# Tokens gathered for two experts at once, in 256 columns, between the down products of the expert before

## The chip, the cores and the metric

The kernel runs on one core of a Trainium2 chip. The metric is device time in microseconds (us), the median of a few executions. Everything is float32 at the interface.

## What is computed

Four transformer layers over 256 tokens of 1024 values. Only the last layer's feed-forward part is touched by the change: a mixture of eight experts, of which each token takes two.

```python
def swiglu(x, w13, w2):
    a, g = jnp.split(x @ w13, 2, axis=-1)
    return (jax.nn.silu(a) * g) @ w2

def moe_ffn(x, router_w, router_b, w13, w2):
    logits = (x @ router_w).astype(jnp.float32) + router_b.astype(jnp.float32)
    top_v, top_i = lax.top_k(logits, TOP_K)
    wts = jax.nn.softmax(top_v, axis=-1)
    gate = jnp.einsum('bsk,bske->bse', wts, jax.nn.one_hot(top_i, N_EXPERTS, dtype=jnp.float32)).astype(x.dtype)
    y = jnp.zeros_like(x)
    for e in range(N_EXPERTS):
        y = y + gate[..., e:e + 1] * swiglu(x, w13[e], w2[e])
    return y
```

An expert's weights are 1024 x 7168 and 3584 x 1024.

## The kernel before

**Precision.** Every operand of a product is split into a high part and a rest, both fp32r. ScalarE writes the high part (`wh`, L1042), VectorE subtracts it from the raw weights (`wl`, L1427), and `t_mm3` (L443 to L445) multiplies high by high, high by rest and rest by high. SyncE loads the weights in slots of 1024 KB (L2239) into a ring of five buffers; three sets of `wh`/`wl` follow one another. Each set is written when the products of the slot three places earlier are done.

**An expert.** The router finds which tokens go to which expert, and each token's place among that expert's at most 128. The kernel gathers the tokens of an expert with a 0/1 matrix: `X` (256 tokens, split into XH and XL, stationary) times `SELR` (128 columns, one for each place, moving) gives the tokens' transpose in PSUM, and ScalarE copies it to `GH` and `GL`. So for each expert TensorE does 8 groups of 128 features x 2 halves of the tokens x 2 parts = 32 matmuls of 128 columns. Then:

- the hidden products, 7 chunks of 512 columns with 4 slots each (12 matmuls of 512 columns in a slot). After a chunk, `turn` transposes the chunk before (4 transposes, L629), and one entry of the list `between` runs;
- the down products, 14 slots, accumulated in two PSUM banks that are held all that time;
- the scatter of the result back to the tokens (`t_scatter`, 2 x 4 matmuls of 512 columns with `SELT`, the transpose of `SEL`), in the first two chunks of the next expert.

**The order** is written out by hand for each engine. `t_experts` (L996) fills `between` for expert e with the scatter of e-1 (chunks 0 and 1), an empty entry, and four pieces of the gather for e+1: 8 matmuls each, after chunks 3 to 6 (1 to 4 in expert 0). The last one also transposes `SEL` (L982, 2 transposes). ScalarE (`a_gather`, L1366) and VectorE (`v_gather`, L2072; both 0/1 matrices of an expert are written in one chunk by `v_choose`, L2065) have lists of the same length. The gather for expert 0 stands alone between the router and the first product, followed by `t_most`, 4 small matmuls. `GH`, `GL`, `SEL`, `SELR` and `SELT` are doubled, by e modulo 2.

**The banks.** `Groups.take` (L164) hands out the eight PSUM banks in turn and makes TensorE wait until the bank's last contents were read:

```python
g = self.n
self.n += 1
self.number[key] = g
if g >= 8:
    engine.wait_ge(self.out_sem[g % 8], g // 8)
return self.banks[g % 8]
```

A second page of experts (for more than 128 tokens at one expert) stands behind a branch that these inputs don't take.

## Time and profile before

| | |
|---|---|
| median of 3 runs | 2379.91 us (2378.08 to 2380.12) |
| the profiled execution's own time | 2378.64 us |
| its span | 2377.2 us |
| TensorE busy | 2330.3 us (98%), weight loads 2002.4 us |
| VectorE busy | 1743.6 us (73%) |
| ScalarE busy | 1375.3 us (58%) |
| read from memory | 577.42 MB |
| chain that ended last | PE 88%, DVE 7%, all others 1% or less |

The own time of the profiled execution is 1.4 us above its span and 1.3 us below the median. Busy shares are means over stages: the eight experts take from 1376 to 2360 us of the span. PE is TensorE, PEld its weight loads, DVE VectorE, ACT ScalarE, SP SyncE.

### The profile page before, as it was taken

To read this page: it belongs to the slowest core of one execution; us is meant where nothing else is said; L and a number is where in the kernel's file an instruction comes from. 1 tells how busy PE (TensorE), PEld (TensorE's weight loads), DVE (VectorE), ACT (ScalarE), POOL (GpSimd) and SP (SyncE) were. 2 spreads that over 40 slices of the span, in tenths; PEclk is the share of its full clock that TensorE was granted. 3 is DMA by queue.
4 is the path that set the end of the run, shared out by engine and by line. 5 is a ranking of instruction groups with operands and counts; after the bars stand their busy time and mean duration, and the time that the engine had idled before them with its cause. 6 is when DMAs were issued, how large, how long until landed. Compare 5 with 4: busy or idle time off the path is not lost.

```text
span 2377.2 us, 31162 instructions
## 1 busy us (share of the span) xinstructions
PE 2330.3 (98%) x12658; PEld 2002.4 (84%) x12658; DVE 1743.6 (73%) x2248; ACT 1375.3 (58%) x1797; POOL 75.8 (3%) x91
## 2 busy tenths in 40 slices
PE   8999999999999999999999899999999999999997
PEld 6898888898888999788899888888888888888885
DVE  6757555857555458655655888989898989899997
ACT  5455444554443444444344367777777777777774
POOL 3100001300000000000000000000000000000000
PEclk9999999999999999999999989999999999999999
DMA  7335554426554534555333489999899989898995
GB/s 249 142 142 202 181 194 142 176 72 239 195 181 152 182 120 178 190 182 200 133 124 109 175 332 359 361 353 364 349 368 347 368 347 377 350 370 345 367 363 187
DMA packets 94167, 580.59 MB, mean 244 GB/s; under 512 B 21776, under 2 KB 23104, under 8 KB 24768
## 3 DMA queue, kind: packets, MB, share of 16 engines
q1 hardware_dynamic: 92704, 572.15, 64.1%
q10 hardware_dynamic: 1312, 6.37, 0.7%
q8 instruction: 102, 1.67, 0.3%
q14 instruction: 49, 0.40, 0.0%
HBM read 577.42 MB, written 1.06 MB: 243 GB/s over the span
## 4 chain that ended last, share of the span: by engine, by line
PE 88%; DVE 7%; DMA 1%; ACT 1%; POOL 1%; issue 1%; SPq 0%; DVEq 0%; POOLq 0%
PE bank L443 26%; PE bank L445 26%; PE bank L444 26%; PE bank L440 7%; DVE wl L1427 3%; PE bank L629 2%; DMA raw<-in_ws 1%; PE bank L675 1%; POOL SM L2143 1%; DVE L L1679 1%; ACT wh L1042 1%; DVE X L1526 0%; DVE GT L1741 0%; DVE SM L1459 0%; DVE X L1471 0%
## 5 line engine op out<-in xcount | busy, mean ns | idle before, releaser
L1427 DVE TENSOR_TENSOR wl<-raw,wh 128x1024 fp32r<-128x1024 f32 x706 | 830.8, 1225 | 233.8 <-ACT wh L1042 232.1
L1042 ACT ACTIVATE wh<-raw 128x1024 fp32r<-128x1024 f32 x706 | 706.4, 1054 | 341.0 <-PE bank L445 299.2
L443 PE MATMUL bank<-wh,GH 128*128 128x512 f32 x896 | 352.1, 393 | 0.0
L445 PE MATMUL bank<-wh,GL 128*128 128x512 f32 x896 | 349.5, 390 | 0.0
L444 PE MATMUL bank<-wl,GH 128*128 128x512 f32 x896 | 349.5, 390 | 0.0
L1427 DVE TENSOR_TENSOR wl<-spare,wh 128x1024 fp32r<-128x1024 f32 x264 | 309.9, 1221 | 22.4 <-ACT wh L1042 21.9
L1042 ACT ACTIVATE wh<-spare 128x1024 fp32r<-128x1024 f32 x264 | 264.5, 1054 | 65.0 <-PE bank L445 65.0
L443 PE MATMUL bank<-wh,HH 128*128 128x512 f32 (+1 forms) x768 | 290.8, 379 | 11.3 <-DVE HL L1442 5.7
L444 PE MATMUL bank<-wl,HH 128*128 128x512 f32 (+1 forms) x768 | 288.3, 375 | 0.0
L445 PE MATMUL bank<-wh,HL 128*128 128x512 f32 (+1 forms) x768 | 287.8, 375 | 0.0
L443 PE MATMUL bank<-HH,wh 128*128 128x256 f32 x896 | 257.4, 287 | 1.7 <-DVE HL L1983 1.7
L445 PE MATMUL bank<-HH,wl 128*128 128x256 f32 x896 | 253.5, 283 | 0.0
L444 PE MATMUL bank<-HL,wh 128*128 128x256 f32 x896 | 253.4, 283 | 0.0
L445 PEld LDWEIGHTS bank<-wh,GL 128*128 128x128 f32 x896 | 168.6, 188 | 35.7
L443 PEld LDWEIGHTS bank<-wh,GH 128*128 128x128 f32 x896 | 168.7, 188 | 34.2
L444 PEld LDWEIGHTS bank<-wl,GH 128*128 128x128 f32 x896 | 168.8, 188 | 34.0
L443 PEld LDWEIGHTS bank<-wh,HH 128*128 128x128 f32 x768 | 146.4, 191 | 40.3 <-issue 8.7
L443 PEld LDWEIGHTS bank<-HH,wh 128*128 128x128 f32 x896 | 171.7, 192 | 5.7 <-issue 2.9
L443 PE MATMUL bank<-wh,EH 128*128 128x512 f32 x448 | 175.8, 392 | 0.0
L445 PE MATMUL bank<-wh,EL 128*128 128x512 f32 x448 | 174.5, 389 | 0.0
L444 PE MATMUL bank<-wl,EH 128*128 128x512 f32 x448 | 174.3, 389 | 0.0
L444 PEld LDWEIGHTS bank<-HL,wh 128*128 128x128 f32 x896 | 171.8, 192 | 0.1
(241 smaller groups left out, 3343.4 us busy)
## 6 DMA issues: line engine op xcount, KB each, us to landing
raw<-in_ws SPq DMA_DIRECT2D x353, 1024.0 KB, 5.1
spare<-in_ws SPq DMA_DIRECT2D x132, 1024.0 KB, 5.9
more<-in_ws SPq DMA_DIRECT2D x48, 1024.0 KB, 4.8
once<-in_ws SPq DMA_DIRECT2D x4, 1024.0 KB, 11.3
QT<-in_relb SPq DMA_DIRECT2D x4, 768.0 KB, 12.5
LNB<-in_ln ACTq DMA_DIRECT2D x3, 1024.0 KB, 4.6
LNB<-in_ln ACTq DMA_DIRECT2D x4, 512.0 KB, 3.5
raw<-in_ws SPq DMA_DIRECT2D x2, 816.0 KB, 4.6
```

What stands on the lines that cost most here:

```text
L440: return T.q.matmul(o, l, r, start=start, stop=stop)
L443: T.q.matmul(o, l[0], r[0], start=start, stop=False)
L444: T.q.matmul(o, l[0], r[1], start=False, stop=False)
L445: return T.q.matmul(o, l[1], r[0], start=False, stop=stop)
L629: ins = T.q.transpose(room[:, 128 * k:128 * k + 128], TU[t][:, 128 * k:128 * k + 128], ident)
L675: ins = T.q.transpose(room[:, 128 * n:128 * n + 128], LB[t][:, 256 * h + 128 * i:256 * h + 128 * i + 128], ident)
L1042: A.q.activation(sets[c % NSET][0][:, half * i:half * i + half], raws[stream.place[n]][:, half * i:half * i + half], ACT.Copy).then_inc(*h ...
L1427: V.q.tensor_tensor(wl[:, half * i:half * i + half], raw[:, half * i:half * i + half], wh[:, half * i:half * i + half].bitcast(f32), ALU.s ...
L1679: ins = V.q.tensor_tensor_reduce(L[:, 256 * h:256 * h + n], room[:, 256 * i:256 * i + n], bias(h), 1.0, NEG if sinks is None else sinks[:, ...
L2143: return G.q.tensor_tensor(o, x, PW[:, 0:x.shape[1]], ALU.pow)
```

## The change

- `t_gather(p)` gathers for the pair of experts 2p and 2p+1 side by side. The moving operand is 256 columns of `SELR`, both experts' matrices next to one another: 32 matmuls of 256 columns for a pair, in eight pieces of 4, each filling one bank.
- For pairs 1 to 3 the pieces stand in the down products of the odd expert ahead of them, one after each of the slots 2 to 9 (`between` of `t_down`). ScalarE copies a piece (128x2x2x128 now) after it has split the slot behind. The hidden products carry no gather.
- `SEL` is transposed for two experts at once (`t_turn_sel`, 4 transposes), in a chunk of the even expert.
- VectorE writes the four 0/1 matrices of a pair one per chunk, in chunks 2 to 5 of the odd expert before. For pair 0 all four are written ahead of expert 0.
- `GH`, `GL`, `SEL`, `SELR`, `SELT` are single arrays that hold a pair, of the same size in all.
- `Groups` counts the uses of each bank, and `skip(2)` lets the ring step over the two banks held by the down products before the sixth piece.

```diff
@@ class Groups
-        self.number, self.n, self.emptied = {}, 0, []
+        self.number, self.at, self.uses, self.emptied = {}, 0, [0] * 8, []
+    def again(self):
+        self.at, self.uses = 0, [0] * 8
+    def skip(self, n):
+        self.at += n
     def take(self, engine, *key):
-        g = self.n
-        self.n += 1
-        self.number[key] = g
-        if g >= 8:
-            engine.wait_ge(self.out_sem[g % 8], g // 8)
-        return self.banks[g % 8]
+        b = self.at % 8
+        self.at += 1
+        self.number[key] = b, self.uses[b]
+        if self.uses[b]:
+            engine.wait_ge(self.out_sem[b], self.uses[b])
+        self.uses[b] += 1
+        return self.banks[b]
     def bank(self, *key):
-        return self.banks[self.number[key] % 8]
+        return self.banks[self.number[key][0]]
...
@@ t_down
                     t_free(s_, full(name, i, tiles - 1, 1))
                 if k0 == 0 and after_first:
                     after_first()
+                if 2 <= k0 // 2 < 2 + len(between):
+                    between[k0 // 2 - 2]()
...
@@ t_gather, t_turn_sel, t_experts
-        def t_gather(e):
-            i = e % 2
-            def move(v, src, c4):
-                room = groups.take(T, "ga", e, v, c4)
+        def t_gather(p):
+            def move(c2, v):
+                room = groups.take(T, "ga", p, v, c2)
                 for t in range(2):
-                    T.wait_ge(*(tokens_in.at(t) if v else part.at("xs", t)))
-                    T.wait_ge(*selr.at(e, t))
-                for c in range(4 * c4, 4 * c4 + 4):
+                    T.wait_ge(*((tokens_in if v else part).at(*([t] if v else ["xs", t]))))
+                    for i in range(2):
+                        T.wait_ge(*selr.at(2 * p + i, t))
+                for j in range(2):
                     for t in range(2):
-                        a = 1024 * t + 128 * c
-                        ins = t_mm(room[:, 128 * (c % 4):128 * (c % 4) + 128], src[:, a:a + 128],
-                                   SELR[i][:, 128 * t:128 * t + 128], t == 0, t == 1)
-                ins.then_inc(*groups.fill("ga", e, v, c4))
-            def last():
-                move(1, XL, 1)
-                room = groups.take(T, "sel", e)
+                        a = 1024 * t + 256 * c2 + 128 * j
+                        ins = t_mm(room[:, 256 * j:256 * j + 256], (XL if v else XH)[:, a:a + 128],
+                                   SELR[:, 256 * t:256 * t + 256], t == 0, t == 1)
+                ins.then_inc(*groups.fill("ga", p, v, c2))
+            return [lambda c2=c2, v=v: move(c2, v) for c2 in range(4) for v in range(2)]
+        def t_turn_sel(p):
+            room = groups.take(T, "sel", p)
+            for i in range(2):
                 for t in range(2):
-                    T.wait_ge(*select.at(e, t))
-                    ins = T.q.transpose(room[:, 128 * t:128 * t + 128], SEL[i][:, 128 * t:128 * t + 128], ident)
-                ins.then_inc(*groups.fill("sel", e))
-            return [lambda: None, lambda: move(0, XH, 0), lambda: move(0, XH, 1), lambda: move(1, XL, 0), last]
+                    T.wait_ge(*select.at(2 * p + i, t))
+                    a = 256 * i + 128 * t
+                    ins = T.q.transpose(room[:, a:a + 128], SEL[:, a:a + 128], ident)
+            ins.then_inc(*groups.fill("sel", p))
         def t_scatter(e, t):
-            i = e % 2
-            w = SELT[i][:, 128 * t:128 * t + 128]
-            T.wait_ge(*out("sel", e))
+            a = 256 * (e % 2) + 128 * t
+            w = SELT[:, a:a + 128]
+            T.wait_ge(*out("sel", e // 2))
             for h in range(2):
                 room = groups.take(T, "sca", e, t, h)
                 T.wait_ge(*out("dn", ("e", e), 0, h))
...
                 t_mm(room[:, :], w, YL[:, 512 * h:512 * h + 512], False, True).then_inc(*groups.fill("sca", e, t, h))
         def t_experts(page):
-            for go in t_gather(8 * page):
+            for go in t_gather(4 * page):
                 go()
             if page == 0:
                 t_most()
             for e in range(8 * page, 8 * page + 8):
-                between = []
+                between, later = [], []
                 if e % 8:
                     between += [lambda t=t: t_scatter(e - 1, t) for t in range(2)]
-                if e % 8 < 7:
-                    between += t_gather(e + 1)
-                turn = t_swiglu(expert_slot(e), GV[e % 2], lambda k, t: out("ga", e, 1, k // 4),
+                if e % 2 == 0:
+                    between += [lambda: t_turn_sel(e // 2)]
+                elif e % 8 < 7:
+                    later = t_gather(e // 2 + 1)
+                    sixth = later[5]
+                    def past():
+                        groups.skip(2)
+                        sixth()
+                    later[5] = past
+                turn = t_swiglu(expert_slot(e), GV[e % 2], lambda k, t: out("ga", e // 2, 1, k // 2),
                                 E_CHUNKS, 1, ("e", e), between)
-                t_down(expert_slot(e) + 28, EV, lambda k, t: out("tu", ("e", e), k // 4, 0), 28, "dn", ("e", e), 1, turn)
+                t_down(expert_slot(e) + 28, EV, lambda k, t: out("tu", ("e", e), k // 4, 0), 28, "dn", ("e", e), 1, turn,
+                       between=later)
...
@@ a_gather, a_experts
-        def a_gather(e):
-            i = e % 2
-            def move(v, dst, c4):
-                a_copy(dst[i][:, 512 * c4:512 * c4 + 512], ("ga", e, v, c4), 512)
-            def last():
-                move(1, GL, 1)
-                a_copy(SELT[i][:, :], ("sel", e), 256)
-            return [lambda: None, lambda: move(0, GH, 0), lambda: move(0, GH, 1), lambda: move(1, GL, 0), last]
+        def a_gather(p):
+            def move(c2, v):
+                A.wait_ge(*full("ga", p, v, c2))
+                A.q.activation((GL if v else GH)[:, :].rearrange("p (i c n) -> p c i n", i=2, c=8)[:, 2 * c2:2 * c2 + 2],
+                               groups.bank("ga", p, v, c2)[:, :].rearrange("p (c i n) -> p c i n", c=2, i=2), ACT.Copy,
+                               scale=1.0).then_inc(*groups.empty("ga", p, v, c2))
+            return [lambda c2=c2, v=v: move(c2, v) for c2 in range(4) for v in range(2)]
...
                 for j in range(14):
                     a_hi(expert_slot(e) + 28 + j + 2)
                     if j == 0:
                         turn()
+                    if 3 <= j < 3 + len(later):
+                        later[j - 3]()
...
@@ v_choose, v_gather
-        def v_choose(e, dst, mark):
+        def v_choose(e, mark):
+            p = e // 2
             V.wait_ge(*out("pos"))
-            for t in range(2):
-                V.q.tensor_scalar(dst[:, 128 * t:128 * t + 128], CST[:, C_ROW:C_ROW + 128], 128.0 * (e // 8) + 1.0,
+            if p:
+                V.wait_ge(*(out("ga", p - 1, 1, 3) if mark is selr else out("sel", p - 1)))
+            for t in range(2):
+                if mark is selr:
+                    dst = SELR[:, 256 * t + 128 * (e % 2):256 * t + 128 * (e % 2) + 128]
+                else:
+                    dst = SEL[:, 256 * (e % 2) + 128 * t:256 * (e % 2) + 128 * t + 128]
+                V.q.tensor_scalar(dst, CST[:, C_ROW:C_ROW + 128], 128.0 * (e // 8) + 1.0,
                                   POS[:, 8 * t + e % 8:8 * t + e % 8 + 1], ALU.add, ALU.is_equal).then_inc(*mark.mark(e, t))
-        def v_gather(e):
-            i = e % 2
-            def choose():
-                v_choose(e, SELR[i], selr)
-                v_choose(e, SEL[i], select)
-            return [choose] + [lambda: None] * 4
...
@@ v_experts
-                if e % 8 < 7:
-                    between += v_gather(e + 1)
                 if e == 0:
-                    between[1] = v_gates_end
+                    between += [lambda: None, v_gates_end]
+                if e % 2 and e % 8 < 7:
+                    between += [lambda x=x, m=m: v_choose(x, m) for m in (selr, select) for x in (e + 1, e + 2)]
```

In the hunks the functions of the same name stand in the order of the file; blank lines are left out.

**Where the instructions now stand.** First TensorE between the router and expert 0. Before:

```order
L440 MATMUL bank<-SM,CST 128x8 x3
L440 MATMUL bank<-SELR_82,XH 128x128 x16
L440 MATMUL bank<-SELR_82,XL 128x128 x16
L982 MATMUL bank<-CST,SEL_80 128x128 x2
L440 MATMUL bank<-SM,CST 128x8 x2
L443 MATMUL bank<-wh,GH_76 128x512
```

Now:

```order
L446 MATMUL bank<-SM,CST 128x8 x3
L446 MATMUL bank<-SELR,XH 128x256 x4
L446 MATMUL bank<-SELR,XL 128x256 x4
...
L446 MATMUL bank<-SM,CST 128x8 x2
L449 MATMUL bank<-wh,GH 128x512
L450 MATMUL bank<-wl,GH 128x512
```

Of the second and third row there are four each, in turns. The gather still has 32 matmuls, of twice the columns, and the transposes of `SEL` are no longer ahead of the first product.

Second, TensorE in the hidden products of expert 1, where a chunk ends. Before:

```order
L443 MATMUL bank<-wh,GH_77 128x512
L444 MATMUL bank<-wl,GH_77 128x512
L445 MATMUL bank<-wh,GL_79 128x512
L629 MATMUL bank<-CST,TU_63 128x128 x4
L440 MATMUL bank<-SELR_82,XH 128x128 x8
L443 MATMUL bank<-wh,GH_77 128x512
```

Now, at the end of such a chunk:

```order
L449 MATMUL bank<-wh,GH 128x512
L450 MATMUL bank<-wl,GH 128x512
L451 MATMUL bank<-wh,GL 128x512
L637 MATMUL bank<-CST,TU_63 128x128 x4
L449 MATMUL bank<-wh,GH 128x512
```

and in its down products, at the end of slot 2:

```order
L451 MATMUL bank<-wh,EL 128x512
L446 MATMUL bank<-SELR,XH 128x256 x4
L449 MATMUL bank<-wh,EH 128x512
L450 MATMUL bank<-wl,EH 128x512
L451 MATMUL bank<-wh,EL 128x512
```

The block of 8 has left the chunk; a block of 4 stands directly between products of 512 columns.

Third, VectorE in expert 1, chunks 2 and 3. Before:

```order
L1442 TENSOR_TENSOR EL<-bank,EH 128x512
L2069 TENSOR_SCALAR SELR_82<-CST,SM 128x128 x2
L2069 TENSOR_SCALAR SEL_80<-CST,SM 128x128 x2
L1576 TENSOR_TENSOR TU_63<-TT_60,bank 128x512
L1427 TENSOR_TENSOR wl<-raw,wh 128x1024 x6
```

Now:

```order
L1461 TENSOR_TENSOR EL<-bank,EH 128x512
L2097 TENSOR_SCALAR SELR<-CST,SM 128x128 x2
L1595 TENSOR_TENSOR TU_63<-TT_60,bank 128x512
L1446 TENSOR_TENSOR wl<-raw,wh 128x1024 x6
L1446 TENSOR_TENSOR wl<-spare_82,wh 128x1024 x2
```

Four writes in one chunk became two in each of four chunks.

## Rows read from the trace of the kernel before

**Rows 1.** Waits, 1380 to 2370 us: engine line <- releaser: total us, times, longest

```profile
ACT wh L1042 <- PE bank L445: 165.4, 235, 2.6
...
SPq L2239 <- DVE wl L1427: 852.5, 325, 18.2
```

**Rows 2.** Busy time by stretch: us, PE, PEld, DVE, ACT, POOL (instructions); clock; DMA share; GB/s

```profile
1510.44:1633.59 123.15, 123.15 (x575) 102.60 (x575) 111.57 (x109) 94.36 (x105) 0.00 (x0) 1.00 0.95 360
...
2249.19:2357.50 108.31, 108.31 (x492) 89.64 (x491) 96.60 (x92) 78.79 (x87) 0.00 (x0) 1.00 0.84 321
...
1364.00:1380.00 16.00, 14.40 (x60) 13.52 (x60) 12.27 (x27) 4.74 (x9) 0.00 (x0) 0.51 1.01 424
```

**Rows 3.** Timeline of TensorE, experts 6 and 7: start us, us, engine, line, operation

```profile
2126.04 0.39 PE L440 MATMUL bank<-YH,SELT 128*128 128x512 f32 x1
...
2238.09 0.39 PE L445 MATMUL bank<-wh,EL 128*128 128x512 f32 x1
...
2249.19 0.39 PE L440 MATMUL bank<-YH,SELT 128*128 128x512 f32 x1
...
2357.51 0.39 PE L445 MATMUL bank<-wh,EL 128*128 128x512 f32 x1
```

**Rows 4.** Timeline of TensorE where products of 256 and 512 columns meet

```profile
1174.75 0.39 PE L445 MATMUL bank<-wh,HL 128*128 128x512 f32 x1
1174.97 0.28 PE L443 MATMUL bank<-HH,wh 128*128 128x256 f32 x1
1175.09 0.28 PE L444 MATMUL bank<-HL,wh 128*128 128x256 f32 x1
...
183.60 0.40 PE L443 MATMUL bank<-wh,MH 128*128 128x512 f32 x1
...
184.99 0.39 PE L443 MATMUL bank<-wh,MH 128*128 128x512 f32 x1
```

**Rows 5.** Timeline of TensorE: small matmuls in a row at the full clock

```profile
1545.70 0.60 PE L629 MATMUL bank<-CST,TU 128*128 128x128 f32 x4
1546.05 1.09 PE L440 MATMUL bank<-SELR,XH 128*128 128x128 f32 x8
...
862.63 3.62 PE L440 MATMUL bank<-U,raw 128*128 128x256 f32 x16
```

**Rows 6.** Timeline, router to expert 0

```profile
1367.72 0.48 DVE L2069 TENSOR_SCALAR SELR<-CST,SM 128x128 fp32r<-128x128 f32 x2
1368.12 1.22 DVE L2017 TENSOR_TENSOR XL<-X,XH 128x1024 fp32r<-128x1024 f32 x1
...
1368.35 3.65 PE L440 MATMUL bank<-SELR,XH 128*128 128x128 f32 x16 [0.95 <-DVE SELR L2069]
...
1369.64 4.63 DVE L1427 TENSOR_TENSOR wl<-raw,wh 128x1024 fp32r<-128x1024 f32 x4
...
1375.21 0.65 PE L982 MATMUL bank<-CST,SEL 128*128 128x128 f32 x2
1375.65 0.86 PE L440 MATMUL bank<-SM,CST 128*128 128x8 f32 x4
1376.36 0.77 PE L443 MATMUL bank<-wh,GH 128*128 128x512 f32 x1
...
1380.08 0.40 PE L443 MATMUL bank<-wh,GH 128*128 128x512 f32 x1
```

**Rows 7.** Busy time by stretch of 1 us: where the clock rises

```profile
1171.00:1172.00 1.00, 1.00 (x4) 0.79 (x4) 0.00 (x0) 0.00 (x0) 0.00 (x0) 0.74 0.12 41
...
1374.00:1375.00 1.00, 1.00 (x7) 1.00 (x6) 0.87 (x5) 0.34 (x1) 0.00 (x0) 0.50 1.03 434
...
1379.00:1380.00 1.00, 1.00 (x4) 0.79 (x3) 1.00 (x2) 0.00 (x0) 0.00 (x0) 0.64 1.02 426
```

**Rows 8.** Timeline before that rise, and VectorE in chunk 2 of expert 1

```profile
1167.63 0.77 PE L443 MATMUL bank<-wh,HH 128*128 128x512 f32 x1 [1.85 <-DVE HL L1442]
...
1536.20 0.47 DVE L2069 TENSOR_SCALAR SELR<-CST,SM 128x128 fp32r<-128x128 f32 x2
```

More of the change, by code:

```diff
@@ L2031, in v_router @@
             V.q.tensor_tensor(POS, groups.bank("pos")[:, 0:16], sm["se"], ALU.mult).then_inc(*groups.empty("pos"))
-            v_choose(0, SELR[0], selr)
+            for e in range(2):
+                v_choose(e, selr)
             v_tokens(1)
-            v_choose(0, SEL[0], select)
+            for e in range(2):
+                v_choose(e, select)
             v_lo(expert_slot(0) + 1)
@@ L2090, in v_experts @@
             if page:
-                for go in v_gather(8 * page):
-                    go()
+                for e in (8, 9):
+                    v_choose(e, selr)
+                for e in (8, 9):
+                    v_choose(e, select)
             for e in range(8 * page, 8 * page + 8):
```

36 lines of the change are left out of this document (19 added, 17 removed).

## The prediction

> **What bounds the kernel now.** The page says that TensorE is busy 98% of the span and has 88% of the chain that ended last, but that is a mean over stages, so I read the experts by themselves. First the waits of that stage [rows 1]. ScalarE waits 165.4 us in 235 waits for a product to free a weight set, the longest 2.6 us; SyncE waits 852.5 us for VectorE to free a buffer. Both run ahead of TensorE. No wait of TensorE is of any size. Then the stretches [rows 2]: from one scatter to the next, 123.15 us, TensorE is busy for all of it at the full clock, VectorE 111.57 us, the DMA engines 95%. So in the experts whatever TensorE no longer issues comes off the time, as long as VectorE, ScalarE and the DMAs keep up. Expert 7 is the test of that, since it has nothing to gather: TensorE is busy without a gap there too. Last I read how tightly small matmuls follow one another [rows 3 to 5], and the start of expert 0 [rows 6, 7], which runs at half the clock.
>
> **Part 1, gather and transposes leave seven experts.** From the first scatter to the last down product, expert 6 takes 2238.09 - 2126.04 = 112.05 us and expert 7 takes 2357.51 - 2249.19 = 108.32 us [rows 3]. They differ by four gather blocks and the two transposes of `SEL`: 3.73 us. Experts 0 to 6 each have them: 7 x 3.73 = **26.1 us removed**. One block takes nearly 0.9 us, as its 8 matmuls follow at (1.09 - 0.28) / 7 = 0.116 us [rows 5].
>
> **Part 2, pieces in the down products.** A piece is 4 matmuls of 256 columns between products of 512. The rows show all three steps [rows 4]: the first 256-column matmul starts 0.22 us after a 512-column one, as another 512 would; 256-column ones follow each other at 0.12 us; and six intervals of 512 after such a stretch take 184.99 - 183.60 = 1.39 us, 0.03 above six times 0.227. So twice the columns cost hardly more than 0.116, and a piece adds 4 x 0.12 + 0.03 = 0.51 us; I take 0.52. The bounds: 4 x 0.116 = 0.46 below; above, 0.60, if a piece leaves the product behind it late by 0.1. With 3 pairs x 8 pieces: 24 x 0.52 = **12.5 us added** (11.1 to 14.4).
>
> The Trainium skill ("TensorE: Matmul & The Clock Gate", section "Back-to-back issue gap") puts a matmul of 128 columns with its weight load at about 81 ns and the isolated gap of 256 columns at N/2.4 + 2.5, some 109 ns. By that, an estimate from the page, 28 blocks of 8 x 81 ns would be 18 us and 24 pieces of 4 x 109 ns 10.5 us, a gain of 7.7 us where the rows give 13.6. The trace does not agree for the small form: 116 ns, not 81.
>
> **Part 3, transposes of SEL.** Four at a time, in experts 0, 2, 4 and 6. Behind `turn`, four follow at (0.60 - 0.27) / 3 = 0.11 us [rows 5], 0.44 us a group; in expert 0 they stand alone, 0.48. **1.8 us added.** Their copy on ScalarE is one of 512 columns in place of two of 256; ScalarE has 123.15 - 94.36 = 28.8 us free in an expert [rows 2].
>
> The experts: -26.1 + 12.5 + 1.8 = **-11.8 us**.
>
> **Part 4, before the first product.** Two more writes of `SELR` stand ahead of the gather: 1368.12 - 1367.72 = 0.4 us for two [rows 6], so the gather starts near 1368.75, and its second piece, which now needs XL, may wait 0.1 us more. At the half clock 32 matmuls of 128 columns follow at 0.215 us ((3.65 - 0.43) / 15 for the first 16). At 1.2 GHz 256 columns also need 256 / 1.2 = 0.213 us, so that clock alone makes the gather no longer. The transposes of `SEL` (1375.65 - 1375.21 = 0.44 us) leave. Late writes and lost transposes cancel: the first product would start at 1376.4, as now.
>
> But the clock may change. It stays at half through 7 us of 128-column gathers that are busy all the time, and rises only in 1379 to 1380, about 3.1 us after the products of 512 columns began; another rise came 3.9 us after such products began, 1167.63 to about 1171.5 [rows 6 to 8]. A 128-column matmul streams 128 / 1.2 = 0.107 us of its 0.215 us; a product of 512 streams all the time, and so would one of 256. I therefore expect the rise 3 to 4.3 us after the gather starts, near 1372.5. About 17 matmuls are then done; the other 15 take 1.8 us, `t_most` 0.4 us in place of 0.71, and the first product starts near 1374.8: 1.6 us earlier. The nine products from 1376.36 to 1380.08 take 3.72 us where the full clock gives 9 x 0.227 = 2.04: another 1.7 us. **-3.3 us** (-2.7 to -3.7). The first slot's rests are ready by then: VectorE wrote those of two slots from 1369.64 in 4.63 us [rows 6]; with four 0/1 writes more ahead of them it starts at 1370.4, and is through with the first slot at 1372.8 and with the second at 1375.1, when that is 2.4 us from its turn.
>
> **What costs nothing, and its cover.** VectorE's 0/1 matrices: before, four writes stood in chunk 2 (from 1536.20 [rows 8], 0.2 us each), which has no gather either, and TensorE did not wait; now at most two stand in a chunk. Expert 7's chunks without a gather leave VectorE idle for 108.31 - 96.60 = 11.7 us in all [rows 2], more than 1 us in a chunk and its share of the down products. If that cover were gone, `wl` would be late next. ScalarE copies as many banks of 512 columns as before, out of 28.8 us that it has free in an expert; each copy stands behind a split that starts as the piece does, so it finds the bank full. If it were late, the next slot's `wh` would be. Banks: the sixth piece steps over the held two, to a bank read since the first down slot.
>
> **The sum.** 2378.64 - 11.8 - 3.3 = 2363.5 us for the profiled execution. The median shown is 1.3 us above it: **2364.8 us**.
>
> **Rivals.**
>
> (a) *The clock does not rise in the gather.* For it: no row shows 256 columns at the half clock. Against: the share of time they stream. Then part 4 is nil: 2379.9 - 11.8 = 2368.1 us. Chance 0.28.
>
> (b) *256 columns cost double.* Matmuls of 256 float32 columns with another operand do: 16 of them take 3.62 us, (3.62 - 0.38) / 15 = 0.216 us apiece [rows 5]. Then 24 pieces take 24 x (4 x 0.216 + 0.03) = 21.5 us, 9 more: 2374 us. Against: `SELR` and `XH` are fp32r, as the operands in rows 4. Chance 0.03.
>
> (c) *Memory sets the pace.* 42 transfers of 1.049 MB in 123.15 us are 358 GB/s; without gathers an expert of 119.4 us needs 369. If 358 were the limit, the experts would keep their 984 us: 2379 us. Against: 424 GB/s moved for 16 us while TensorE ran slow [rows 2]. The Trainium skill ("DMA: Bandwidth & Descriptors", section "Where 436 GB/s comes from") names about 358 GB/s as what memory gives one core, which is the pace of now to the digit. By that rule this change gains nothing; the 424 GB/s speak against it. Chance 0.03.
>
> (d) *Slower: VectorE is the hidden bound of the hidden products.* It is busy 9 parts in 10 [rows 2], and the gathers were time in which it caught up. If hidden stretches kept their length, the pieces would be added in three experts and nothing taken away: +12.5 - 3.3, some 2389 us. It decides once VectorE falls back by more than its lead within one expert's hidden products. That lead is some 3 us: a set is freed two slots of 12 x 0.227 = 2.72 us ahead of its use, and the first halves of split and rest take some 2.3 of these 5.4 us (1.16 for the rest [rows 6], as much assumed for the split). Expert 7 shows none of it. Chance 0.03.
>
> **How the numbers follow.** Forecast 0.60, (a) 0.28, (b), (c) and (d) 0.03 each, 0.03 for what I don't see. The forecast's bounds are 24 x 0.06 = 1.4 us down with 0.4 us of clock, and 24 x 0.08 = 1.9 us up with 0.6; (a) with its upper bound reaches 2370. With a microsecond of spread between runs, the range is 2362.5 to 2370.5. What can be told from no change is about 0.2%, 4.8 us. The forecast and (a) are faster by more, (b) by 6 us too: 0.91. Within 0.2%: (c) and part of the unseen, 0.05. Slower: 0.04.
>
> **What would show it.** From scatter to scatter, even experts take 123.15 - 3.73 + 0.44 = 119.9 us and odd ones 123.15 - 3.73 + 4.2 = 123.6 us, TensorE busy throughout. 256-column gathers follow at 0.12 us, pieces add 0.52. The granted clock is 1.00 before 1374. Wrong would be: TensorE waiting for `wl` in hidden products (d), ScalarE for a DMA (c), a clock of 0.50 up to 1379 (a), gathers at 0.2 us in the down products (b).

## The result, and the profile after

| | before | after |
|---|---|---|
| median | 2378.99 us (4 runs, 2374.81 to 2380.12) | 2360.81 us (4 runs, 2357.62 to 2363.02) |
| profiled execution's own time | 2378.64 us | 2357.62 us |
| its span | 2377.2 us | 2356.3 us |
| TensorE busy | 2330.3 us | 2310.0 us |
| VectorE, ScalarE busy | 1743.6, 1375.3 us | 1738.8, 1371.7 us |

By the medians of these four and four runs the changed kernel is faster by 18.2 us; the ratio on record is 0.9929, with a 95% interval of 0.9918 to 0.9941 (14 to 20 us). The forecast was 2364.8 us in a range of 2362.5 to 2370.5: the direction holds, the time lies 1.7 us below the range. With all executions of both unchanged kernels in this study the medians are 2377.1 us (71 runs, 2373.7 to 2382.3) and 2361.0 us (9 runs, 2357.6 to 2363.0), 16.2 us apart (2377.11 and 2360.96).

The stretches of the experts first, from one scatter to the next (busy time by stretch, columns as in [rows 2]; an odd expert, an even one, expert 7, and last the 16 us from the start of the gather):

```profile
1499.46:1622.91 123.45, 123.45 (x574) 102.66 (x572) 111.55 (x113) 95.54 (x109) 0.00 (x0) 1.00 0.96 359
1622.91:1742.74 119.83, 119.83 (x545) 99.31 (x544) 110.50 (x105) 92.16 (x102) 0.00 (x0) 1.00 0.97 370
...
2229.30:2337.64 108.34, 108.34 (x492) 89.65 (x491) 96.58 (x92) 78.79 (x87) 0.00 (x0) 1.00 0.85 322
1364.00:1380.00 16.00, 16.00 (x79) 14.12 (x80) 15.34 (x23) 11.73 (x18) 0.00 (x0) 0.87 1.01 425
```

The forecast was 123.6 and 119.9 us where all experts took 123.15 before; expert 7, which had no gather and has none, is unchanged. TensorE is busy for all of each stretch. In the last row the granted clock is 0.87 over the first 16 us from the gather. The row of [rows 2] with 0.51 begins 4.35 us ahead of its gather; over the 16 us from its own gather, at 1368.35, the kernel before had 0.64:

```profile
1368.35:1384.35 16.00, 16.00 (x66) 14.49 (x67) 12.56 (x18) 7.33 (x12) 0.00 (x0) 0.64 1.01 424
```

The waits from 1375 to 2350 us, to set beside [rows 1]:

```profile
ACT wh L1060 <- PE bank L451: 161.0, 232, 1.6
DVE wl L1446 <- ACT wh L1060: 62.3, 154, 0.9
```

ScalarE still waits for TensorE to free weight sets. No wait of TensorE for rests and none of ScalarE for a transfer has come in.

A piece in the down products (timeline of TensorE, columns as in [rows 3]):

```profile
1577.88 0.39 PE L451 MATMUL bank<-wh,EL 128*128 128x512 f32 x1
1578.11 0.64 PE L446 MATMUL bank<-SELR,XH 128*128 128x256 f32 x4
1578.58 0.40 PE L449 MATMUL bank<-wh,EH 128*128 128x512 f32 x1
1578.82 0.40 PE L450 MATMUL bank<-wl,EH 128*128 128x512 f32 x1
...
1581.33 0.64 PE L446 MATMUL bank<-SELR,XL 128*128 128x256 f32 x4
```

From piece to piece it is 1581.33 - 1578.11 = 3.22 us. Of that 12 products take 12 x 0.227 = 2.72, so a piece costs 0.50 us; 0.52 was forecast.

Router to expert 0 (timeline, to set beside [rows 6]; in brackets the idle time before, and what ended it):

```profile
1355.12 1.97 PE L471 MATMUL bank<-CST,X 128*128 128x128 f32 x8 [2.73 <-DVE X L1490]
...
1364.00 1.20 PE L446 MATMUL bank<-SELR,XH 128*128 128x256 f32 x4 [1.34 <-DVE SELR L2097]
1365.14 1.20 PE L446 MATMUL bank<-SELR,XL 128*128 128x256 f32 x4
...
1369.43 0.64 PE L446 MATMUL bank<-SELR,XL 128*128 128x256 f32 x4
...
1370.27 0.47 PE L449 MATMUL bank<-wh,GH 128*128 128x512 f32 x1
```

The clock over the same stretch (busy time by stretch of 1 us; the third number from the right is the granted clock):

```profile
1367.00:1368.00 1.00, 1.00 (x6) 1.00 (x6) 1.00 (x2) 0.60 (x1) 0.00 (x0) 0.50 1.03 434
1368.00:1369.00 1.00, 1.00 (x10) 1.00 (x9) 1.00 (x2) 0.92 (x2) 0.00 (x0) 0.90 0.99 418
```

A piece takes 1.05 to 1.20 us from its first start to its last end at half the clock and 0.64 at the full one. The clock rises near 1368.2, some 4.2 us after the gather began and 2.1 us before the first product.

Measured from event to event, the two profiled executions compare so (us). The first products stand in [rows 6] and above, the last ones at 2357.51 [rows 3] and 2337.64 us; the tail is the span less that, and as spans are given to 0.1 us it is good to 0.05.

| stretch | before | after | difference | forecast |
|---|---|---|---|---|
| start to the router's second transposes (unchanged code) | 1359.86 | 1355.12 | -4.74 | 0 |
| from there to the first product | 16.50 | 15.15 | -1.35 | -1.6 |
| first to last product | 981.15 | 967.37 | -13.78 | -13.5 |
| last product to the end (unchanged code) | 19.69 | 18.66 | -1.03 | 0 |

Where the kernel was changed, it gained 15.13 us, and 15.1 were forecast (-1.6 is the first half of part 4; -13.5 is its second half, 1.7, and the experts' 11.8). The rest of the surplus stands in code that the change doesn't touch, and that is where the experiments start.

### The profile page after: what moved, and what is told of

It is laid out like the page before. It is cut to its first block, busy times and chain, and to the rows that moved or that the text cites. A ratio compares the mean times of both kernels' runs of the same rounds, so it can differ in the third digit from the quotient of the medians.

```text
span 2356.3 us, 30894 instructions
## 1 busy us (share of the span) xinstructions
PE 2310.0 (98%) x12530; PEld 1982.8 (84%) x12530; DVE 1738.8 (74%) x2248; ACT 1371.7 (58%) x1793; POOL 75.3 (3%) x91
## 4 chain that ended last, share of the span: by engine, by line
PE 88%; DVE 7%; DMA 1%; ACT 1%; POOL 1%; issue 1%; SPq 0%; DVEq 0%; POOLq 0%
PE bank L449 26%; PE bank L451 26%; PE bank L450 26%; PE bank L446 6%; DVE wl L1446 3%; PE bank L637 2%; DMA raw<-in_ws 1%; PE bank L683 1%; POOL SM L2165 1%; DVE L L1698 1%; ACT wh L1060 1%; DVE X L1545 0%; DVE GT L1760 0%; DVE SM L1478 0%; DVE X L1490 0%
```

## The experiments

Twelve kernels. In every profile I read the same four stretches. The time of the router's second transposes is called the router's start below.

### Both kernels again, unchanged

> The kernel before, unchanged: a look at how much its first 1360 us, which the change does not touch, differ between two profiled executions of the same program. Theory A (the 3 us that the forecast missed are variation of the clock in unchanged code): the router's second transposes start somewhere between 1354 and 1361 us, not at 1359.9 again to 0.2 us, and the stretches at 59 to 66 us and 948 to 954 us show a clock of 0.5 or 1.00 by chance; from there to the last product it takes 997.6 us again within 0.5. Rival B (something about the program fixes them): 1359.9 again, with the same dips in the clock at the same places. Time 2379 us within 4, ratio 1.000.

> The changed kernel, unchanged. Theory A (variation of the clock in unchanged code): the router's second transposes start between 1354 and 1361 us and not at 1355.1 again; from there to the last product 982.5 us again within 0.5; over more runs the difference of the medians falls to 15 to 16.5 us, 2362.5 to 2364. Rival B (the change does something to the first 1355 us, too): 1355.1 again within 0.2, a clock of 1.00 at 59 to 66 us and at 948 to 954 us, and a difference of 18 us again.

The kernel before again: 2376.86 us (11 runs), ratio 1.0001 (0.9992 to 1.0010) to itself. The changed one: 2361.08 us (5 runs), ratio 0.9934 (0.9921 to 0.9948) to 2377.1 us (27 runs). The router starts at 1360.22 and 1358.21 us; from there to the last product it is 998.51 and 982.69 us. The changed kernel's own repeat starts its router 3.09 us later than its first profile did. Most of that is the granted clock. First the changed kernel's first profile, then its repeat (busy time by stretch of 2 us):

```profile
62.00:64.00 2.00, 2.00 (x11) 1.64 (x10) 2.00 (x3) 0.00 (x0) 1.67 (x2) 1.00 0.86 356
...
948.00:950.00 2.00, 2.00 (x11) 1.58 (x10) 1.34 (x2) 0.00 (x0) 0.00 (x0) 1.00 1.01 287
```

```profile
62.00:64.00 2.00, 2.00 (x6) 1.61 (x5) 2.00 (x2) 0.00 (x0) 2.00 (x3) 0.50 0.68 131
...
950.00:952.00 2.00, 2.00 (x7) 1.60 (x6) 1.92 (x2) 0.00 (x0) 0.00 (x0) 0.60 0.68 160
```

The same instructions run at 2.4 GHz in one execution and partly at 1.2 GHz in the other: 11 matmuls in the two microseconds from 62, or 6. TensorE had been waiting just before. Where it resumes shows how much each place adds (timeline of TensorE: first the kernel before, then the changed kernel's first profile, then its repeat):

```profile
59.49 0.77 PE L443 MATMUL bank<-wh,HH 128*128 128x512 f32 x1 [2.76 <-DVE wl L1427]
949.25 0.50 PE L443 MATMUL bank<-wh,MH 128*128 128x512 f32 x1 [2.54 <-DVE wl L1427]
972.97 1.35 PE L465 MATMUL bank<-CST,X 128*128 128x128 f32 x6 [1.87 <-DVE X L1471]
```

```profile
59.02 0.47 PE L449 MATMUL bank<-wh,HH 128*128 128x512 f32 x1 [2.64 <-DVE wl L1446]
945.99 0.50 PE L449 MATMUL bank<-wh,MH 128*128 128x512 f32 x1 [2.52 <-DVE wl L1446]
968.10 1.75 PE L471 MATMUL bank<-CST,X 128*128 128x128 f32 x8 [1.86 <-DVE X L1490]
```

```profile
60.18 0.47 PE L449 MATMUL bank<-wh,HH 128*128 128x512 f32 x1 [2.78 <-DVE wl L1446]
948.57 0.80 PE L449 MATMUL bank<-wh,MH 128*128 128x512 f32 x1 [2.53 <-DVE wl L1446]
972.07 1.32 PE L471 MATMUL bank<-CST,X 128*128 128x128 f32 x8 [1.87 <-DVE X L1490]
```

The repeat is 1.2 us behind its first profile when TensorE resumes near 60 us, before any dip at that place; no run here explains that part. It is 2.6 us behind near 948 and 4.0 near 970, after the dips at 60 and 950, 1.4 us for each. Then 0.9 us comes back, since the first profile has its clock at one half from 969 to 972 us and the repeat does not. The kernel before was 0.5 us behind the changed one near 60 us, 3.3 near 948 and 4.9 near 970: its dip at 60 us lasts 6.8 us and costs 2.8.

All fourteen profiles, the first two and the twelve here, share this code up to the transposes of the first token tile, 8.2 us ahead of the router's start in every one of them. The dip at 60 to 70 us shows in eleven of them and the one at 940 to 960 in nine; one at 968 to 977 shows in ten, among them all five that have none at 940 to 960. The router starts between 1356.55 and 1360.22 us (mean 1358.3) in the five profiles with the gather of before, and between 1355.12 and 1360.33 (mean 1357.8) in the nine with the new one. Theory A holds, rival B falls: the 4.7 us were one favourable execution set against one unfavourable. The means differ by 0.5 us, a small part of the spread inside either group; that something of it is real can't be excluded with so few.

### The tail: instructions moved, nothing else

The stretch behind the last product was 1.0 us longer before, and 20.07 us again in the repeat, against 18.80 for the repeat of the changed kernel: in both pairs it is there. In `vector_front` of each kernel:

```diff
-            V.q.memset(PT[:, 1024:1536], 0.0).then_inc(*zeroed.mark())
+            for i in range(8):
+                V.q.memset(PT[:, 1024 + 64 * i:1088 + 64 * i], 0.0).then_inc(*zeroed.mark())
```

> The kernel before with VectorE's first memset of 512 columns cut into eight of 64, so that all its later instructions stand seven places further on; nothing else. It is about the 1.0 to 1.3 us gap ahead of the first aggregate of the last norm, which both profiles of the kernel before show (as a wait for nothing that the profile sees) and none of the others. Theory (the gap belongs to where that instruction stands in the program): it is gone or at another instruction, and from the last product to the end it takes 18.7 in place of 19.7 to 20.1 us. Rival (it comes from the work of the kernel before): 19.7 to 20.1 again. Its router start is one more sample of the unchanged part: 1355 to 1361 us.

> The changed kernel with the same eight memsets. Theory (the place of the instruction in the program): from the last product to the end 18.7 us, or a gap of about 1 us that comes back if the shift happens to put it there. Router start 1355 to 1361 us, from there to the last product 982.6 us within 0.8, time 2361 us within 2.

The kernel before with this shift: 2375.64 us (10 runs), ratio 0.9995 (0.9986 to 1.0005), tail 18.69 us. The changed one: 2360.49 us (4 runs), ratio 0.9929 (0.9912 to 0.9945), tail 18.55 us. VectorE behind the last product (timeline), first in the kernel before, then in the same with the shift:

```profile
2364.58 1.29 DVE L1459 BATCH_NORM_STATS2 SM<-X 128x6 f32<-128x512 f32 x2 [2.43 <-issue]
2366.89 0.21 DVE L1462 BATCH_NORM_AGGREGATE SM<-SM 128x2 f32<-128x12 f32 x1 [1.02 <-issue]
```

```profile
2361.19 1.28 DVE L1459 BATCH_NORM_STATS2 SM<-X 128x6 f32<-128x512 f32 x2 [2.34 <-issue]
2362.51 0.21 DVE L1462 BATCH_NORM_AGGREGATE SM<-SM 128x2 f32<-128x12 f32 x1
```

The second wait of 1.02 us ("issue": nothing that the profile shows) is gone. It stands in both profiles of the kernel before (1.0 and 1.3 us) and in none of the twelve others. It is not the work: the shifted kernel and the two below that change only TensorE's and ScalarE's part (`place128`, `no_gather`) have the same work on VectorE behind the last product, and none has the gap. That it belongs to where the instruction stands in the program fits all fourteen profiles, but the test of it by itself, seven instructions more far ahead, is one profile. What VectorE waits for there no run shows. So the changed kernel most likely got this microsecond by having other instructions ahead. The median of the shifted kernel is 0.6 us below that of the kernel before, measured beside it, inside the interval, so it is the profile that bears this out, not the time.

### The place alone, with 128 columns

```diff
@@ t_experts (before)
-                if e % 8 < 7:
-                    between += t_gather(e + 1)
+                later = []
+                if e % 8 < 7:
+                    later = t_gather(e + 1)[1:] + [lambda: groups.skip(2)]
```

`t_down` takes `between=later` as in the changed kernel, and ScalarE's copies move along.

> The kernel before, with its gathers of 128 columns for one expert moved out of the hidden products into the down products of the same expert, slots 2 to 6; width, writes and start as before. Theory (the gain in the experts comes from the width alone, since TensorE never waits): 28 blocks of 8 matmuls cost 0.93 us wherever they stand, so 0 us within 1 of the kernel before, and scatter to scatter 123.15 us again within 0.15. Rival (the place is worth something by itself: gathers in the hidden products cost TensorE more than their own time, or VectorE gets its time back): up to 28 x 0.1 = 3 us less, scatter to scatter 122.7. Rival d turned round (hidden products without gathers become VectorE's): slower by more than 3 us, with waits of TensorE for the rests.

2377.23 us (11 runs), ratio 1.0005 (0.9996 to 1.0014). Scatter to scatter is 123.40 us in all six, 0.25 more than before: outside what the theory allowed (0.15), on the side that no rival had. The timeline of TensorE shows the piece's other end:

```profile
1590.24 0.39 PE L454 MATMUL bank<-wh,EL 128*128 128x512 f32 x1
1590.46 1.00 PE L449 MATMUL bank<-SELR,XH 128*128 128x128 f32 x8
1591.30 0.45 PE L452 MATMUL bank<-wh,EH 128*128 128x512 f32 x1
1591.60 0.40 PE L453 MATMUL bank<-wl,EH 128*128 128x512 f32 x1
```

The second product follows the first by 0.30 us, where products among themselves take 0.227: each return from 128 columns to 512 costs 0.07 us. In the hidden products the block shared that return with the transposes of `turn`; alone in the down products it pays its own, 0.25 us over four blocks in an expert, 0.06 each, 1.7 us in all. (The median does not show it, since this kernel's tail is 1.2 us shorter than that of the kernel before.) So the place is worth nothing by itself, and even costs a little; the gain in the experts is the width's. A piece of 256 columns returns cheaper (0.24 us, above).

### How much of the gathers was on the path

The kernel before, in which experts 1 to 7 compute with the tokens of expert 0 and gather none (`t_gather` and `a_gather` issue only the transposes of `SEL` and their copy):

```diff
+            if e % 8:
+                return [lambda: None] * 4 + [lambda: last(False)]
             return [lambda: None, lambda: move(0, XH, 0), lambda: move(0, XH, 1), lambda: move(1, XL, 0), last]
```

> The kernel before without the gathers of experts 1 to 7 (28 blocks of 8 matmuls and their copies on ScalarE); these experts compute with the tokens gathered for expert 0, so that part of the computation is left out. SEL is still transposed for each. It tells how much of the gathers' time was on the path. Theory (TensorE never waits in the experts, so all of it was): 7 x (3.73 - 0.22) = 24.6 us less than the kernel before, scatter to scatter 123.15 - 3.51 = 119.64 us. Rival c (memory sets the pace at 358 GB/s): no change, 123 us, and waits of ScalarE for transfers. Rival d (VectorE bounds the hidden products once the gathers leave them): less than 24.6 by 5 us or more, with waits of TensorE for the rests.

2350.77 us (4 runs), ratio 0.9879 (0.9863 to 0.9896). Router's start to last product 973.19 us against 997.94, the mean of the kernel before in three profiles (997.65, 998.51 and 997.66 with the shift): -24.75 us, where 24.6 were expected. The median's 27.9 us hold the tail's microsecond, too; some 2 us of them these stretches do not explain. One expert (busy time by stretch):

```profile
1624.20:1743.84 119.64, 119.64 (x544) 99.08 (x542) 111.17 (x109) 91.96 (x102) 0.00 (x0) 1.00 0.97 369
```

119.64 us to the hundredth, TensorE without a gap, memory at 369 GB/s. All of a gather's time was on the path, and neither memory nor VectorE set in below 123 us: rival (c) falls here by itself, and so does (d) for hidden products without a gather.

### What a piece costs

In `t_gather` of the changed kernel the products of a piece are issued twice for pairs 1 to 3:

```diff
+                for again in range(2 if p else 1):
+                    for j in range(2):
+                        for t in range(2):
...
```

> The changed kernel with each of the 24 pieces in the down products issued twice over (the same products, written again). Theory (a piece costs its own time on TensorE and nothing hides it): 4 x 0.12 = 0.48 us for each second piece, 24 x 0.48 = 11.5 us slower than the changed kernel; scatter to scatter of the odd experts 123.4 + 3.8 = 127.3 us, of the even ones unchanged. Rival (part of a piece's cost is what it does to the product behind it, and its own matmuls take less): between 9 and 11 us. Rival (pieces push VectorE or the memory, which then catch up): less than 9 us.

2372.63 us (7 runs), ratio 0.9970 (0.9958 to 0.9981). First scatter to last product takes 849.80 us against 838.23 (838.18 and 838.28): 11.57 more, 0.482 us a piece, and odd experts take 127.27 us. The doubled piece:

```profile
1584.80 1.12 PE L446 MATMUL bank<-SELR,XL 128*128 128x256 f32 x8
1585.75 0.40 PE L449 MATMUL bank<-wh,EH 128*128 128x512 f32 x1
```

Eight matmuls in 0.95 us. The theory holds; the rest of the 0.50 us is the return to 512 columns.

### VectorE's cover

Extra 0/1 writes to spare memory ahead of each write for pairs 1 to 3 (two, or six):

```diff
+        def v_more(e, mark, t):
+            for i in range(6):
...
+                V.q.tensor_scalar(SPOTS[m % 8][:, :], CST[:, C_ROW:C_ROW + 128], 128.0 * (e // 8) + 1.0,
...
```

> The changed kernel with each 0/1 write of VectorE for pairs 1 to 3 made three times over (the extra ones go to spare memory): 0.94 us more of VectorE in each of chunks 2 to 5 of the odd experts. It measures the cover that rival d of the prediction is about. VectorE is idle for 0.5 us of such a chunk of 11.3 us now, so it falls back by 0.44 us a chunk, 1.8 us in all, inside the lead of some 3 us. Theory (the lead is 3 us): 0 us slower than the changed kernel, within 0.5. Rival (the lead is near nothing): 3 x 1.8 = 5.3 us slower.

> The same with seven writes in place of one: 2.8 us more of VectorE in each of four chunks. It falls back by 2.3 us a chunk, 9.3 us in all. Theory (a lead of some 3 us): 6.3 us lost in each of three odd experts, 19 us slower than the changed kernel, with waits of TensorE for the rests. Rival (no lead): 28 us slower. Rival (a lead of two slots and more, 6 us): 10 us slower.

With two more: 2360.72 us (4 runs), scatter to scatter 123.42 us, nothing lost. With six more: 2379.55 us (10 runs), ratio 1.0007 (0.9997 to 1.0017) to the kernel before; odd experts 129.55, 129.52 and 129.55 us, 18.4 us more from the first scatter to the last product, where 19 were expected. Waits from 1375 to 2350 us there:

```profile
ACT wh L1062 <- PE bank L453: 178.3, 232, 2.4
...
PE bank L451 <- DVE wl L1448: 13.9, 12, 1.4
```

The second row is the wait that rival (d) was about. Here all of the gain would have gone.

The lead of 3 us does not come out of it. The expectation has VectorE falling back by 9.3 us an expert, from 2.8 us of writes in a chunk, and 9.3 less the 6.1 us lost would be 3.2. But the timeline (rows of VectorE, and the last of TensorE) has the writes follow at (1530.15 - 1528.98) / 6 = 0.195 us, so twelve more are 2.3 us a chunk and 9.4 us an expert before VectorE's idle time is taken off:

```profile
1528.98 1.26 DVE L2093 TENSOR_SCALAR SPOT<-CST,SM 128x128 fp32r<-128x128 f32 x6
1530.15 0.28 DVE L2109 TENSOR_SCALAR SELR<-CST,SM 128x128 fp32r<-128x128 f32 x1
...
1532.32 1.22 DVE L1448 TENSOR_TENSOR wl<-raw,wh 128x1024 fp32r<-128x1024 f32 x1
1533.93 0.39 PE L452 MATMUL bank<-wl,GH 128*128 128x512 f32 x1
```

The last two rows are a half of a set's rests and the first product with it: written by 1533.54, used at 1533.93, 0.39 us later, where TensorE had to wait. The same half in the changed kernel (again a row of each engine):

```profile
1526.39 1.22 DVE L1446 TENSOR_TENSOR wl<-raw,wh 128x1024 fp32r<-128x1024 f32 x1
1529.67 0.39 PE L450 MATMUL bank<-wl,GH 128*128 128x512 f32 x1
```

It is written by 1527.61 and used 2.06 us later, the shortest distance in an odd expert. So the lead is some 1.7 us (2.06 less 0.39), about half of what the prediction had worked out; an estimate, since it takes the 0.39 us as the least that is possible. With two more writes the shortest distance is 0.99 us (rests from 1566.27 in 1.25 us, the product at 1568.52): VectorE fell back by 1.1 us and not by the 1.8 of the expectation, and 0.6 us was left. The odd experts of the changed kernel have the 1.7 us whole. In expert 0 it is used up: that starts sooner than before, and its shortest distance, at 1398.83, is 0.45 us, where the kernel before had 1.86. TensorE waited for nothing measurable there, but a still sooner start may run into it.

### The gather in 128 columns

```diff
-                    for t in range(2):
...
-                        ins = t_mm(room[:, 256 * j:256 * j + 256], (XL if v else XH)[:, a:a + 128],
-                                   SELR[:, 256 * t:256 * t + 256], t == 0, t == 1)
+                    for i in range(1 if p else 2):
+                        n = 256 if p else 128
+                        for t in range(2):
...
+                            ins = t_mm(room[:, o:o + n], (XL if v else XH)[:, a:a + 128],
+                                       SELR[:, b:b + n], t == 0, t == 1)
```

> The changed kernel, but the gather of the first pair is made in 64 matmuls of 128 columns in place of 32 of 256. Theory (what lets the clock rise in the gather is how much of the time the matmuls stream): the clock stays at one half for all of the gather, 64 x 0.215 = 13.8 us long, and for 3 us of products behind it. The gather then takes 13.8 in place of 5.9 us and the half-clock penalty of 1.7 us is back: 9.6 us slower than the changed kernel. Rival (the clock rises after some 4 us of busy TensorE, whatever it does): 19 matmuls at 0.215 and 45 at 0.116 us, 9.3 us in all: 3.4 us slower.

2371.94 us (11 runs), ratio 0.9979 (0.9970 to 0.9988), 10.9 us above the changed kernel's median, measured beside it. The gather begins at 1364.47 and the first product stands at 1378.97, 14.5 us later. The granted clock (busy time by stretch):

```profile
1377.00:1378.00 1.00, 1.00 (x7) 1.00 (x6) 0.00 (x0) 0.29 (x1) 0.00 (x0) 0.50 1.03 426
...
1381.00:1382.00 1.00, 1.00 (x4) 0.81 (x3) 1.00 (x2) 0.08 (x1) 0.00 (x0) 0.50 1.00 418
1382.00:1383.00 1.00, 1.00 (x5) 0.77 (x5) 1.00 (x2) 0.00 (x0) 0.00 (x0) 0.86 0.64 262
```

TensorE is busy without a gap and stays at 1.2 GHz through 14 us of 128-column gathers, then rises 3.3 us after products of 512 columns began. Router's start to last product is 992.37 us against 982.60, the mean of three: 9.8 more, 9.6 expected, where the rival had 3.4. The rival, a rise after some 4 us of busy TensorE whatever it does, falls. The same gather in 256 columns was followed by the rise 4.1 to 4.4 us after its start in four profiles, and 5.9 us after it in two others (with twice the pieces, and with two more writes of VectorE, neither of which touches this gather). The 128-column gather has twice the matmuls and half the width, so which of the two keeps the clock down this run does not tell apart.

### Beyond both kernels: keeping the clock up

```diff
+        def t_keep(room, n, s):
+            for _ in range(n):
+                t_mm(room[:, 0:512], s[:, 0:128], s[:, 512:1024], True, True)
...
+                room = groups.take(T, "rt", t)
                 if t == 1:
+                    t_keep(room, 11, HH)
                     t_turn_x(7, 1)
```

The second kernel has `t_keep(room, 5, XH)` ahead of the first piece, besides.

> The changed kernel with 11 needless matmuls of 512 columns (their result is overwritten) in the 2.7 us in which TensorE waits for the norm ahead of the router's second transposes. They take 11 x 0.227 = 2.5 us at the full clock and should end before the wait does. Theory (the clock falls at 1354.8 because TensorE stood idle from 1352.4): it stays at 1.00 through these transposes, which take 1.0 in place of 2.0 us, and a part of the router; what is left open is whether it stays up through matmuls of 8 and 16 columns and the waits of 0.7 and 1.3 us. If it falls there, 1 to 2 us less than the changed kernel, if it holds, 4 us less. Rival (the clock falls all the same): 0, or up to 1 us slower where the needless matmuls run past the wait.

> The same with 5 more needless matmuls of 512 columns (XH by XH) in the 1.3 us in which TensorE waits for SELR ahead of the gather. If the clock is at 1.00 there, they take 1.1 us, the gather runs at the full clock from its start (4 us in place of 5.9 with its wait for XL) and the whole is 3.5 to 4.5 us less than the changed kernel. If it is at one half there, they take 2.1 us, the gather starts 0.8 us late and the clock rises that much sooner before its end: 0 to 1 us better or worse than with the 11 alone.

2359.14 and 2359.29 us (4 runs each), ratios 0.9922 (0.9906 to 0.9939) and 0.9926 (0.9909 to 0.9942); the changed kernel with the shift, measured beside them, 2360.49. I count from the transposes of the first token tile, which stand ahead of the needless matmuls: to the last product 990.71 and 990.88 us in the changed kernel's two profiles, 989.36 with eleven needless matmuls and 989.00 with sixteen, 1.4 and 1.8 us less. The eleven end before the wait does, so the router starts 8.2 us behind those transposes as in all others. The second kernel (busy time by stretch):

```profile
1359.00:1360.00 1.00, 0.93 (x7) 0.74 (x7) 0.93 (x6) 0.93 (x3) 0.00 (x0) 1.00 0.74 123
1360.00:1361.00 1.00, 0.78 (x6) 0.69 (x6) 1.00 (x2) 0.67 (x1) 0.00 (x0) 0.81 0.73 279
1361.00:1362.00 1.00, 1.00 (x6) 1.00 (x6) 1.00 (x2) 0.00 (x0) 0.00 (x0) 0.50 0.92 385
```

In both the clock holds through the transposes, which take 1.3 us in place of 2.0. In the second kernel it falls near 1360.6, among the router's matmuls of 8 and 16 columns; in the first it stays up through them, to 1364.9, and falls in the wait behind them. Neither has it up at the gather, so the lower of the expected gains came about. The five before the gather run at half the clock and delay it by 1.1 us (gather 8.95 us after the router's start, against 7.83), which the sooner rise gives back. With the eleven alone the rise came 3.6 us after the gather began. The two are the lowest medians of the kernels here that compute everything, but 1.2 to 1.4 us in four runs each is no more than the spread between runs; the profile bears the gain out, the times alone would not.

## Why the prediction was right, and where it was wrong

**The experts (parts 1 to 3): right.** First to last product 13.8 us less, with 13.5 forecast. Part 1 priced 28 blocks from the difference of experts 6 and 7 [rows 3]; leaving the blocks out gave back 24.75 us of 24.6. Part 2's 0.52 us for a piece measures 0.50, and 0.48 for a second one right behind. Part 3's 0.44 us for a group of `SEL` transposes was not tested alone; it fits the even experts, 119.83 to 119.90 us in different profiles, where by estimate 119.42 would be left with neither gather nor transposes (119.64 less half of 0.44), so 0.41 to 0.48. The Trainium skill ("TensorE: Matmul & The Clock Gate", section "Back-to-back issue gap") would by the prediction's estimate have given 7.7 us for the blocks and the pieces. The 13.6 us set beside it in the prediction hold the transposes of `SEL`, too, which the estimate leaves out; like for like the rows had 24.6 - 12.5 = 12.1 us, and the runs gave 24.75 - 24 x 0.50 = 12.75. The trace does not agree with the page's 81 ns: 128-column matmuls of this kernel follow at 0.11 to 0.12 us.

**The start (part 4): right, with a spread that it did not have.** 0.4 us for two more writes (router's start to gather 8.49 and 8.88 us), the clock's rise about 4 us after the gather began, the first product at full clock; -1.35 us where -1.6 stood, and the half-clock penalty gone behind it. That the clock would rise in a gather of 256 columns and not in one of 128 held in both halves: with 128 columns it was at half for 14 us, and 9.8 us were lost. What was a chance of 0.28, (a), fell. The penalty that was priced at 1.7 us is not fixed: in the kernels with the old gather the rise came 3.4 to 3.6 us after the first product in four profiles and 5.1 us after it in the repeat of the kernel before, which makes 0.85 us more. The changed kernel has such a spread, too, ahead of the first product: in the two profiles with the rise 5.9 us after the gather's start, the first product stands 15.9 us after the router's start, not 15.2. That the compared pair had the shorter case on both sides is luck.

**The rivals.** (b) is out by the 0.12 us of a 256-column matmul. (c) is out: the experts without gathers ran at 369 GB/s, the even experts of the changed kernel at 370, with no wait of ScalarE for a transfer. The trace doesn't agree with the Trainium skill ("DMA: Bandwidth & Descriptors", section "Where 436 GB/s comes from") that some 358 GB/s is what memory gives one core; the section has the figure as one of two cores' shares, and here one core ran. That the old pace had the same number was chance: it went up to 369 when TensorE had less to do. (d) did not happen, but its mechanism is real: 9.4 us more of VectorE's work in each odd expert turned the gain to nothing. The lead with which the prediction set it aside, some 3 us, was too high. The shortest lead in the odd experts is some 1.7 us, and in expert 0 hardly any is left. The prediction's working left out VectorE's other work of a chunk, which stands ahead of the rests of one slot in four; there the lead is shortest.

**The step that failed** is the last one, "The median shown is 1.3 us above it: 2364.8 us", and with it "With a microsecond of spread between runs, the range is 2362.5 to 2370.5". The sum itself, -15.1 us, was taken off a level that was too high, and the range was narrower below than what the unchanged code does by chance. In numbers:

- The level. Three runs gave 2379.91 us. Over 71 runs the median is 2377.11, with 8 in 10 of them between 2374.8 and 2379.9 us. That alone is 2.8 us of the 4.0 us by which the forecast lies too high. The profiled execution had its router's start at 1359.86 us, when the five profiles with the old gather give 1358.3 in the mean. Its clock was 0.988, and the rows at 60, 950 and 970 us would have shown that dips there were part of its time.
- The tail. A wait of 1.0 to 1.3 us at one instruction of the kernel before went away, most likely because the program ahead of it changed. It stood in the trace before the change, as a wait for nothing visible, and was read as part of the work.
- The rest is within the terms: router's start to last product -15.34 us in the mean of three profiles each (the shifted kernels' with them), where -15.1 was forecast.

Together, -15.34 and -1.15 (tails of 19.88 and 18.73 us in the mean of the two profiles of each kernel) make -16.5 us, and the medians of all runs lie 16.2 us apart.

## What to carry to other kernels

Where one engine is busy without a gap, price a change by the start-to-start times of its instructions in the trace: such a sum held to 0.3 us in 15, and so did the terms that were tested alone. A lead of one engine over another is better read from the trace at its shortest place than worked out: here that gives 1.7 us for 3. Small gathers are cheaper wide than many, and their place matters only for what stands next to them. The level from which the sum is taken needs as much care as the sum: read where the granted clock dips in unchanged code and which waits for nothing visible stand in the profiled execution, count both as things that may come and go, and let the range reach over them.

## What the runs showed of the hardware

- The same program, on the same data, starts its router up to 3.1 us apart. TensorE's clock was 1.2 GHz for 3.4 us or more behind 60, 950 and 970 us in some executions and 2.4 GHz in others; a dip of 3.4 us costs about 1.4 us at the first two places, and 1.2 of the 3.1 us arise ahead of the first. All three places follow a wait of TensorE of 1.9 to 2.8 us.
- 14 us of back-to-back matmuls of 128 columns ran at 1.2 GHz to their end. With 256 columns the clock rose 3.6 to 5.9 us after their start, with 512 columns 3.3 to 5.1 us after.
- The return from 128-column matmuls to products of 512 delays the second product by 0.07 us more than going on with 512, from 256 columns by 0.01 (0.03 over the products behind).
- A wait of 1.0 to 1.3 us on VectorE behind the last product stood in both profiles of one program and in none of twelve others, one of which differs from that program in seven more small instructions far ahead.
- Experts of the same instructions repeated their length to 0.08 us between programs and executions: at the full clock the time of TensorE is not what varies.
- Where TensorE waited for a rest that VectorE wrote, its first product with it started 0.39 to 0.46 us after VectorE's last write.
